# State-space scan of a hybrid decoder trunk: decay segments from running sums that are read back as rows, and the output scaled by a diagonal matrix inside its transpose

## The reference

```python
def step(state, inp):                       # one chunk of Q = 128 tokens
    xc, dtc, bc, cc = inp
    cum = jnp.cumsum(dtc * A, axis=1)
    seg = cum[:, :, None] - cum[:, None]
    L = jnp.exp(jnp.where(tril, seg, -jnp.inf))
    xdt = xc.astype(f32) * dtc[..., None]
    cb = jnp.einsum('btgn,bsgn->btsg', cc, bc)
    y_diag = jnp.einsum('btsgh,bsghp->btghp', cb[..., None] * L, xdt)
    y_off = jnp.einsum('btgn,bghpn->btghp', cc, state) * jnp.exp(cum)[..., None]
    decay = jnp.exp(cum[:, -1:] - cum)
    new_state = (state * jnp.exp(cum[:, -1])[..., None, None]
                 + jnp.einsum('bsgn,bsghp->bghpn', bc, xdt * decay[..., None]))
    return new_state, y_diag + y_off
...
yg = (y.reshape(B, S, SSM_D_INNER) * jax.nn.silu(z)).reshape(B, S, G, SSM_D_INNER // G)
yg = yg * lax.rsqrt(jnp.mean(yg * yg, axis=-1, keepdims=True) + EPS)
y = yg.reshape(B, S, SSM_D_INNER) * norm_w
return y @ w_out
```

## Time and profile before

| what | value |
|---|---|
| time, median of 3 runs | 1568.55 us (1567.23 to 1568.96) |
| the profiled execution: its own time / its span | 1567.98 us / 1566.1 us |
| PE busy in it | 1494.7 us (95%) |
| PEld / DVE / ACT / POOL busy | 1212.5 / 863.1 / 576.5 / 290.0 us |
| the scan (its four groups) in the span | 939.67 to 1149.01 us |
| DMA moved | 130.68 MB, mean 83 GB/s |

### The profile page before, as it was taken

How to read it: one execution, slowest core, us unless ns; L and a number is a source line. 1 busy time by engine, 2 the same in 40 slices (tenths; PEclk the granted TensorE clock), 3 DMA queues, 4 the chain that set the end, 5 groups by cost and what they waited for, 6 DMA issues and landing times.

```text
span 1566.1 us, 19940 instructions
## 1 busy us (share of the span) xinstructions
PE 1494.7 (95%) x7469; PEld 1212.5 (77%) x7469; DVE 863.1 (55%) x1119; ACT 576.5 (37%) x864; POOL 290.0 (19%) x325
## 2 busy tenths in 40 slices
PE   6979899899999999999999999998999999999999
PEld 4768777677788888788788867776787888887887
DVE  4546767665544444333397758989646444444222
ACT  4446666554423222222233353344333222232110
POOL 4154443400300000000000025666212000000000
PEclk9989999999999999999999999999999999999999
DMA  8200100111232222332232220111122223222232
GB/s 318 81 28 1 55 28 28 64 72 58 78 107 87 100 100 87 108 108 94 94 108 81 83 105 27 55 54 39 69 81 81 95 93 107 83 105 93 95 107 80
DMA packets 19737, 130.68 MB, mean 83 GB/s; under 512 B 2272, under 2 KB 2912, under 8 KB 5088
## 3 DMA queue, kind: packets, MB, share of 16 engines
q1 hardware_dynamic: 19536, 127.80, 23.1%
q10 hardware_dynamic: 144, 2.10, 0.4%
HBM read 127.79 MB, written 2.10 MB: 83 GB/s over the span
## 4 chain that ended last, share of the span: by engine, by line
PE 80%; POOL 9%; issue 6%; DVE 2%; ACT 1%; POOLq 0%; DVEq 0%; ACTq 0%
PE ps L431 22%; PE ps L432 22%; PE ps L433 22%; PE ps L732 4%; POOL Lx L2034 3%; PE ps L712 2%; PE ps L692 2%; POOL sqacc L1940 1%; POOL sm L1926 1%; POOL xdd L2029 1%; PE ps L636 1%; PE ps L637 1%; POOL xdt L2026 1%; PE ps L708 1%; POOL qn L1978 1%
## 5 line engine op out<-in xcount | busy, mean ns | idle before, releaser
L1386 DVE TENSOR_TENSOR wl<-wraw,wh 128x2048 fp32r<-128x2048 f32 x113 | 263.6, 2333 | 236.8 <-ACT wh L999 236.6
L431 PE MATMUL ps<-xh,wh 128*128 128x512 f32 (+2 forms) x912 | 359.1, 394 | 6.8 <-DVE xl L1396 3.4
L433 PE MATMUL ps<-xh,wl 128*128 128x512 f32 (+2 forms) x912 | 356.1, 390 | 0.0
L432 PE MATMUL ps<-xl,wh 128*128 128x512 f32 (+2 forms) x912 | 355.9, 390 | 0.0
L999 ACT ACTIVATE wh<-wraw 128x2048 fp32r<-128x2048 f32 x113 | 215.5, 1907 | 186.7 <-PE ps L433 177.8
L431 PEld LDWEIGHTS ps<-xh,wh 128*128 128x128 f32 (+2 forms) x912 | 170.6, 187 | 44.9 <-issue 4.5
L433 PEld LDWEIGHTS ps<-xh,wl 128*128 128x128 f32 (+2 forms) x912 | 170.5, 187 | 37.3
L432 PEld LDWEIGHTS ps<-xl,wh 128*128 128x128 f32 (+2 forms) x912 | 170.5, 187 | 36.7 <-issue 0.7
L431 PE MATMUL ps<-hh,wh 128*128 128x512 f32 x352 | 137.9, 392 | 4.1 <-DVE hid L1471 4.1
L432 PE MATMUL ps<-hl,wh 128*128 128x512 f32 x352 | 137.8, 391 | 0.0
L433 PE MATMUL ps<-hh,wl 128*128 128x512 f32 x352 | 137.6, 391 | 0.0
(11 more groups left out here) (274 smaller groups left out, 2444.6 us busy)
## 6 DMA issues: line engine op xcount, KB each, us to landing
wraw<-wstream SPq DMA_DIRECT2D x113, 1024.0 KB, 4.7
cw<-cw_in SPq DMA_DIRECT2D x1, 4096.0 KB, 18.6
xT<-xT_in SPq DMA_DIRECT2D x4, 512.0 KB, 8.1
part<-xT_in ACTq DMA_DIRECT2D x1, 2048.0 KB, 7.6
out<-xT SPq DMA_DIRECT2D x8, 256.0 KB, 6.5
rows<-rows_in SPq DMA_DIRECT2D x1, 276.0 KB, 10.7
tri<-tri_in SPq DMA_DIRECT2D x1, 192.0 KB, 9.9
cmask<-cmask_in SPq DMA_DIRECT2D x1, 128.0 KB, 10.1
```

What stands on the lines that cost most here:

```text
L431: mm(o, wa[0], xa[0], start=start, stop=False)
L432: mm(o, wa[0], xa[1], start=False, stop=False)
L433: return mm(o, wa[1], xa[0], start=False, stop=stop)
L1386: TTo(wl[:, s, :], wraw[:, s, :], wh[:, s, :].bitcast(F32), ALU.subtract).then_inc(lo_done, 1)
```

## The change

The differences of running sums are no longer made by PE. The running sums of all 128 chunk-head pairs (`cum`, from the first of three products that were there before) are copied to SBUF, transposed once, written to a DRAM tensor `cum_rows` (128x128), and read back for each chunk as eight rows broadcast to all partitions (`rowc`, 512 KB, two buffers, issued from ACT's queue two chunks ahead). ACT makes `seg = relu(cum_s - row)` head by head (eight instructions of 128x128, with a column of `cum` as bias), and `Lx = exp(-seg)` from SBUF. `build_g` and the two PE products go. `scale_y` writes the diagonal matrix `ydiag = ident * rstd` (128x128) and leaves `ybuf` as it is; `to_features` multiplies each block of `ybuf` by it, as a float32 product where a transpose stood.

With it come changes of order and of banks. `z_part` alternates between banks 0 and 5, `half_product` goes round banks 5, 0, 1. At the end of a group, DVE does `split_lo` behind `y_done` and not ahead of it. At chunk 0 of the last group ACT makes `yh`, and DVE `yl`, ahead of the rest of that chunk. `split_hi(n0 + 2)` stands ahead of the first `decays`. `chunk_F` waits for all eight `half_copy`.

```diff
-        Gm = a.take("Gm", [P, 2, 4, P])
+        seg = a.take("seg", [P, 2, 4, P])
+        rowc = a.take("rowc", [P, 2, SHP, P])
...
         def half_bank(t):
-            return 6 if t == 6 else 5
+            return (5, 0, 1)[t % 3]
+        def z_bank_of(tt):
+            return 5 if tt % 2 else 0
...
# PE
-            def decays(g, j):
-                for q in range(2):
-                    pe.wait_ge(g_built, g * 8 + (2 * j + q + 1))
-                    after(pe, seg_exp, g * 8 + (2 * j + q - 1))
-                    mm(ps[:, q, :], tri[:, 1, :], Gm[:, q, :, :].rearrange("p h t -> p (h t)"), start=True, stop=True
-                       ).then_inc(seg_mm, 1)
+            def chunk_products(g, j):
                 pe.wait_ge(staged, g * 4 + (j + 1))
...
                 for f in range(4):
-                    ins = pe.transpose(ps[:, 7, f * P:(f + 1) * P], ybuf[:, j % 2, f * P:(f + 1) * P], ident[:, :])
+                    ins = mm(ps[:, 7, f * P:(f + 1) * P], ybuf[:, j % 2, f * P:(f + 1) * P], ydiag[:, j % 2, :],
+                             start=True, stop=True)
...
-                        pe.wait_ge(evac, g * 4 + (t0 + 4 + tt))
+                        pe.wait_ge(evac, g * 4 + (t0 + 4 + tt - 1))
...
-                    after(pe, half_stored, t if t < 6 else t - 1)
+                    after(pe, half_stored, t - 2)
...
+            pe.wait_ge(cum_copied, 1)
+            pe.transpose(ps[:, 7, 0:P], cum[:, :], ident[:, :]).then_inc(cumT_mm, 1)
             pe.wait_ge(cum_exp, 1)
-            decays(0, 0)
+            pe.wait_ge(cumT_done, 1)
+            chunk_products(0, 0)
...
                 def free(m):
+                    if c == 0:
+                        pe.wait_ge(half_stored, 8)
...
# ACT
+            act.wait_ge(cumT_done, 1)
+            act.dma_start(cum_rows, cumT[:, :]).then_inc(rows_stored, 16)
...
             def decays(g, j):
+                at_ = g * SHP + ((j // TT) * SHP + (j % TT) * SH)
+                act.wait_ge(row_landed[j % 2], g * 32 + 16 * (j // 2 + 1))
                 for q in range(2):
-                    act.wait_ge(seg_mm, g * 8 + (2 * j + q + 1))
+                    after(act, seg_exp, g * 8 + (2 * j + q - 1))
+                    for h in range(4):
+                        ins = A(seg[:, q, h, :], rowc[:, j % 2, 4 * q + h, :], ACT.Relu, scale=-1.0,
+                                bias=cum[:, bass.ds(at_ + 4 * q + h, 1)])
+                    ins.then_inc(seg_built, 1)
+                for q in range(2):
+                    act.wait_ge(seg_built, g * 8 + (2 * j + q + 1))
                     after(act, y_mm, g * 8 + 2 * (j - 1))
-                    A(Lx[:, j % 2, q, :, :], ps[:, q, :].rearrange("p (h t) -> p h t", h=4), ACT.Exp
-                      ).then_inc(seg_exp, 1)
+                    A(Lx[:, j % 2, q, :, :], seg[:, q, :, :], ACT.Exp, scale=-1.0).then_inc(seg_exp, 1)
+                if not isinstance(g, int) or 4 * g + j + 2 < 4 * SG:
+                    row_load(g, j + 2)
+            def row_load(g, j):
+                at_ = g * SHP + ((j // TT) * SHP + (j % TT) * SH)
+                act.dma_start(rowc[:, j % 2, :, :], cum_rows[bass.ds(at_, SHP), :].unsqueeze(0).broadcast_to([P, SHP, P])
+                              ).then_inc(row_landed[j % 2], 16)
...
             stage(0, 1)
+            act.wait_ge(rows_stored, 16)
+            row_load(0, 0)
+            row_load(0, 1)
+            split_hi(n0 + 2)
             decays(0, 0)
-            split_hi(n0 + 2)
...
# DVE
             def scale_y(g, j):
                 dve.wait_ge(y_rs, g * 4 + (j + 1))
-                y = ybuf[:, j % 2, :]
-                TS(y, y, yst[:, j % 2, 2:3], None, ALU.mult).then_inc(y_scaled, 1)
+                after(dve, yT_mm, g * 4 + (j - 1))
+                TS(ydiag[:, j % 2, :], ident[:, :], yst[:, j % 2, 2:3], None, ALU.mult).then_inc(y_scaled, 1)
...
-                    if k < 2 or not last:
-                        build_g(g, k + 2)
-                    if k == 3 and not last:
-                        split_lo(n0 + 4, g, 2)
+                    if last and k == 0:
+                        for kt in range(0, FIRST_KT, 2):
+                            y_lo(kt // 2 + 1, 2 * TT, slice(0, TT), slice(kt, kt + 2))
...
                     TTo(y, y, zs[:, k, :], ALU.mult).then_inc(y_done, 1)
+                    if k == 3 and not last:
+                        split_lo(n0 + 4, g, 2)
```

More of the change, by code:

```diff
@@ L261, in trunk @@
         yst = a.take("yst", [P, 2, 4])
+        ydiag = a.take("ydiag", [P, 2, P])
         a = Region(conv_at)
@@ L1303, in z_copy @@
                     act.wait_ge(z_mm, g * 3 + (tt + 1))
-                A(zraw[:, tt % TT, :], ps[:, 5, :], ACT.Copy, scale=stat[:, 4 + tt % TT:5 + tt % TT]).then_inc(evac, 1)
+                A(zraw[:, tt % TT, :], ps[:, z_bank_of(tt), :], ACT.Copy, scale=stat[:, 4 + tt % TT:5 + tt % TT]).then_inc(evac, 1)
             def group(g, last):
@@ L1315, in group @@
                         split_hi(n0 + 3, g, 2)
+                    if last and k == 0:
+                        stage(g, 2)
+                        act.wait_ge(products, 2 * CHUNK["ssm_out"])
+                        act.wait_ge(yT_done, 2 * TT)
+                        for kt in range(0, FIRST_KT, 2):
+                            A(yh[:, :, kt:kt + 2, :], yT[:, :, kt:kt + 2, :], ACT.Copy).then_inc(yh_done, 1)
                     if last and k >= 2:
@@ L1320, in group @@
                         decays(g, k + 1)
-                    if k < 2 or not last:
+                    if not last or k == 1:
                         stage(g, k + 2)
@@ L1332, in group @@
                     if last and k == 0:
-                        act.wait_ge(products, 2 * CHUNK["ssm_out"])
-                        act.wait_ge(yT_done, 2 * TT)
-                        for kt in range(0, FIRST_KT, 2):
-                            A(yh[:, :, kt:kt + 2, :], yT[:, :, kt:kt + 2, :], ACT.Copy).then_inc(yh_done, 1)
                         split_hi(CHUNK["ssm_out"] + 1)
@@ L1788, in _ @@
             n0 = CHUNK["z"]
-            def build_g(g, j):
-                for q in range(2):
-                    after(dve, seg_mm, g * 8 + (2 * j + q - 1))
-                    at_ = g * SHP + ((j // TT) * SHP + (j % TT) * SH + 4 * q)
-                    TTo(Gm[:, q, :, :], tri[:, 0, :].unsqueeze(1).broadcast_to([P, 4, P]),
-                        dtb[:, 1, bass.ds(at_, 4)].unsqueeze(2).broadcast_to([P, 4, P]), ALU.mult).then_inc(g_built, 1)
             def stage(g, j):
@@ L1874, in group @@
                     TTo(y, y, zs[:, k, :], ALU.mult).then_inc(y_done, 1)
+                    if k == 3 and not last:
+                        split_lo(n0 + 4, g, 2)
                     if k or not first:
                         to_features(g, k - 1)
-                    if last and k == 0:
-                        for kt in range(0, FIRST_KT, 2):
-                            y_lo(kt // 2 + 1, 2 * TT, slice(0, TT), slice(kt, kt + 2))
                     if last and k == 1:
```

30 lines of the change are left out of this document (18 added, 12 removed).

## The result

The changed kernel takes 1547.0 us (median, 1546.31 to 1549.25); the kernel before, on the same chip, 1568.33 us (1567.23 to 1568.96). The ratio is 0.9867, 95% interval 0.985 to 0.9884: 21.3 us less. The forecast's sum gave 1545.3, with 1541 to 1549 as the likeliest case and a range of 1538 to 1553. The profiled execution took 1546.55 us with a span of 1544.7.

The account below looks back on a forecast made before the run. PE was taken to set the pace in the first three groups, with waits in the last. From 1567.98: -27.5 + 1.7 + 6.9 - 2.4 - 8.0 + 2.4 + 3.6 = -23.3, so 1544.7, median 1545.3; range 1538 to 1553.

Parts of the forecast that it names:

- Half clock: Rival, chance 0.2: in the last group, PE's clock falls again after new waits of 2.3 and 1.3 us; +3, 1548.
- The products, -27.5: On PE in the scan: removing the pair of `tri x Gm` products saves 1.72 us in each of 16 chunks.
- the diagonal, +6.9: PE's `to_features`: four float32 products of 0.22 us replace transposes of 0.11, +0.43 us a chunk.
- the banks at -2.4: Loop turns: alternating banks ends PE's two waits for bank 5 (`zraw`), saving 2.4 us.
- the 8.0 of the last group: Last group: waits of 3.3 (`yl`), 1.0 (`Gm`), 0.8 (half product's copy) and half clock of 2.9 go: -8.0.
- +6.0 of new waits: New PE waits: +2.4 at the ends of groups 0, 1 and 2, and +3.6 in the last group.
- the term of +1.7: Scan start: group 0 begins where it began, so 1.7 us PE saves in its first decays are lost waiting.
- The wait for the diagonal at the turns: Ends of groups 0, 1 and 2: PE waits 0.8 us for the scaled diagonal, three times, +2.4.
- The 3.3, 1.0, 0.8: Last group: PE's old waits for `yl`, `Gm` and a half product's copy, forecast to go.
- The 1.15 us for each `yl`: Last group, DVE: each `yl` piece takes 1.15 us, so the 3.3 us wait for `yl` goes.
- The wait for the product with `zs`: Last group: PE waits 2.3 us for the DVE product with `zs`, behind ACT's `yh`, Relus and an issue.
- The case of a longer table switch: Last group, ACT: a table switch costs 2.66 us, making the wait 3.7 and the time 1546.7; chance 0.05.

Follow-up runs that it names:

- the run above: The changed kernel with its order of work around the group turns and its PSUM banks put back, decays by rows and diagonal kept: 1564.46 us, ratio 0.9979.
- The run with `bc` first: The changed kernel with ACT's two staging copies of `bc` for the first group put ahead of its Exp of the running sums and the row store: 1545.44 us.

## Why the prediction was right, and where it was not

**The time and the direction** were right: 1547.0 in 1541 to 1549, the likeliest case. Part of how close it came is luck. In the profiled pair the scan gave 20.1 us where the sum had 23.3, and 1.3 of the rest came from an earlier start of the running sums, which differs from one execution to the next. No rival came true as written. Half clock did come, but in the changed kernel at the start alone, and not in the last group, where I had put it (1.00 there; five of its variants have 0.95 in that group, and three 0.97).

**The products, -27.5, and the diagonal, +6.9.** As PE's work both are right: group 0, where PE waits for nothing before and after, fell by 5.5 us, with 4 x (1.72 - 0.43) = 5.2 worked out. My reading of 44.89 us for that group took in 0.88 of the next, so the 39.2 that I forecast for it came out as 38.47.

**The step that failed is the value given to banks and order.** I argued that PE was busy 44.55 of 45.73 us, "and what PE no longer does there is time saved until another engine's chain is late", and put the banks at -2.4 and, inside the 8.0 of the last group, -0.8: the waits that could be seen. They are worth 11 to 12 us. The order had -6.2 for the `yl` wait and its half clock against +6.0 of new waits, nearly nothing, and is worth 6 to 8. The removal with the diagonal, by itself, is worth 2.3 where the terms give 27.5 - 6.9 - 1.7 + 1.0 = 19.9. What the runs showed in its place: with the products gone and the rest old, PE waits 8.0 us for bank 5 where it waited 2.4, 5.2 for `yl` where it waited 3.3, 3.3 for DVE's output at the state product where it waited 0.5, with half clock behind the long ones. The sum was right because these waits were closed by banks and order in the same change, and I counted them nowhere, neither opened nor closed. A forecast of the removal alone by the same method would have missed by some 17 us; the one made after the result, in the run above, still missed by 8.

**The start.** I had group 0 begin where it began, because PE would wait for ACT's chain of rows, Relus and Silus. In the two traces it does (939.75 against 939.67), but only since the running sums came 1.3 us sooner; counted from them it begins 1.4 later, so the term of +1.7 measures +3.1. The reason was wrong too. ACT's chain was 1 us shorter than I walked it (first Silus at 934.74, eight Relus 2.44), and ACT then waited 2.4 us for PE. PE's own stretch was late: a wait of 0.45, one of 1.33 for `bc`, and then half clock. The run with `bc` first gave 2.5 us back.

**The wait for the diagonal at the turns.** Priced 0.8 each (by my own terms 0.9, as the 7.4 adds up to 7.3); measured 1.2 to 1.35. The step that was mis-sized is 0.2 us for the diagonal on DVE: 0.96 to 1.06, since POOL's `xdt` starts first.

**The last group.** Predicted 66 us to the second half, measured 67.87. The 3.3, 1.0, 0.8 and the half clock did go. The 1.15 us for each `yl` was wrong for the same reason as the diagonal (2.1 each, beside POOL), and gave 2.0 us of waits that I had at none. The wait for the product with `zs`, put at 2.3, came out at 0.3, because PE itself arrived 3.7 us later than worked out and DVE's output, behind the four `yl`, 1.6 later. The scaling of chunk 0 cost 0.87 for 1.3. The case of a longer table switch, given 0.05, did not come: Silu started 0.02 us behind the load.

**ACT and the row loads.** Relus of 389 ns, 0.30 apart: right. ACT has 28.0 to 28.1 us of work per turn where I had 29.8. The loads land in 3.6 us at the median; one took 5.8, beyond the 5 that I had set as a sign of being wrong, and no wait of PE came from it. Nor did the wait for the product with `zs` of 2 to 3 us come, which I had named as a sign of being right.

## What to carry to other kernels

Work on the busiest engine that stands between two uses of one PSUM bank is also the time in which the other engine empties the bank. Before pricing its removal, find on the timeline when that copy ends: the wait that isn't in the list yet is the term. And a short instruction's price is read beside its neighbours: a row of 0.2 to 0.3 us taken where POOL is idle says nothing of the place where POOL has just started one of a microsecond.

## What the runs showed of the hardware that I had not expected

- The scaled diagonal on DVE, started after a POOL instruction, lasts until that one ends, whether TENSOR_SCALAR (288 ns alone, 1057 beside `xdt`) or TENSOR_TENSOR (293 and 1124), and the other way round (on POOL 398 ns, 2067 behind DVE's `wl`). Over the scan (930 to 1127 us of the changed kernel's trace, groups by form with count, busy us and mean ns), the 128x512 instructions with two inputs in SBUF are drawn out (0.69 us for one alone), and those that read PSUM are not:

```profile
L1898 DVE TENSOR_TENSOR ybuf<-ybuf,zs 128x512 f32<-128x512 f32 x16 | 13.6, 848 | 3.1 <-ACT zs L1361 2.6
L1895 DVE TENSOR_TENSOR ybuf<-ybuf,dxs 128x512 f32<-128x512 f32 x12 | 10.7, 896 | 0.4
L1886 DVE TENSOR_TENSOR state<-state,ex 128x512 f32<-128x512 f32 x8 | 9.6, 1197 | 0.0
...
L1884 DVE TENSOR_TENSOR ybuf<-ps,ex 128x512 f32<-128x512 f32 x12 | 8.3, 690 | 29.5 <-PE ps L967 29.5
```

- PE's granted clock fell to 0.50 for about 3 us behind waits of 1.18 and 1.25 us in some traces (first loop turn of the runs with `bc` first and with the diagonal by TENSOR_TENSOR) and not in others with the same wait (1.18 in the change), at a cost of about 1.6 us (42.26 against 40.63 us for the turn). What decides it these runs don't show; the waits of 2.42 and 2.39 in the two turns of the kernel with old order and banks were both followed by it.
